# Front's input projection of a transformer-like block on one Trainium2 core: split fp32r operands in place of plain f32

## The reference, cut to what matters

```
h = x*(1 + scale) + shift ;  z = h @ w_in                      # [1024, P_IN], f32
mlstm:  q, k, v, o, gates   = z[:, 0:4*256], z[:, 1024:1040]
sgu:    u, v                = gelu(z[..., :256]), layer_norm(gelu(z[..., 256:]))
conv:   a = z[..., :256] * sigmoid(z[..., 256:]); 31-tap depthwise convolution in rows of 64 tokens,
        layer norm, silu
s5:     16 groups of a diagonal complex recurrence (64 states, two directions), driven by z[..., -256:]
```

## Time and profile before

| | |
|---|---|
| runs, us | 2306.5 (median), 2300.97, 2306.6 |
| profiled execution: span, us | 2301.7 (the page has no other time of it) |
| PE, DVE, ACT, POOL busy, us | 2196.2 (95%), 1350.5 (59%), 816.3 (35%), 333.9 (15%) |
| L1070, Front's tiles, PE busy us | 169.1, 384 records for 192 matmuls |
| DMA, mean | 94 GB/s |

### The profile page before, as it was taken

The page is one execution under the profiler, slowest core; times in us unless marked ns, Lnnn a source line. Parts: engine busy times, 40 slices in busy tenths (PEclk is TensorE's granted clock), DMA queues, the critical chain, the costliest instruction groups (busy, mean ns, idle before and its releaser), DMA issues. The chain is left out here.

```text
span 2301.7 us, 26756 instructions
## 1 busy us (share of the span) xinstructions
PE 2196.2 (95%) x10489; PEld 1634.2 (71%) x10489; DVE 1350.5 (59%) x2051; ACT 816.3 (35%) x1394; POOL 333.9 (15%) x257
## 2 busy tenths in 40 slices
PE   6999998878999999999999889999999999999999
PEld 3454764466778888888888668996768977444887
DVE  3829948576897655555455685317856387567210
ACT  3100113362562333333434352326544333446110
POOL 1000000031234322220000100004200000364000
PEclk9999999989999999999999999999999999999999
DMA  8531018304534322226534221100131210113331
GB/s 280 168 89 64 28 46 274 128 20 147 150 107 126 96 85 86 84 89 240 183 123 134 65 91 47 37 1 19 62 90 56 56 37 19 74 35 109 83 85 52
DMA packets 215428, 216.76 MB, mean 94 GB/s; under 512 B 18850, under 2 KB 171738, under 8 KB 214376
## 3 DMA queue, kind: packets, MB, share of 16 engines
q1 hardware_dynamic: 200076, 196.57, 27.3%
q0 software_dynamic: 3344, 12.58, 1.5%
q10 hardware_dynamic: 11884, 5.91, 0.9%
HBM read 172.12 MB, written 41.74 MB: 93 GB/s over the span
## 5 line engine op out<-in xcount | busy, mean ns | idle before, releaser
L2360 PE MATMUL bk_in<-t_part,a 128*128 128x512 f32 x1272 | 294.6, 390 | 1.3 <-DVE arena L2835 0.9
L2360 PEld LDWEIGHTS bk_in<-t_part,a 128*128 128x128 f32 x1272 | 238.4, 188 | 53.1 <-issue 3.0
L2379 PE MATMUL bk_in<-hid_part,b_part 128*128 128x512 f32 x1056 | 242.0, 391 | 3.1 <-DVE b_part L2710 3.1
L2379 PEld LDWEIGHTS bk_in<-hid_part,b_part 128*128 128x128 f32 x1056 | 198.1, 188 | 46.3 <-DVE b_part L2710 3.9
L1070 PE MATMUL fr_ps<-arena,work 128*128 128x512 f32 x384 | 169.1, 601 | 5.0 <-DMA work<-in_w_in 5.0
L3166 PE MATMUL bk_in<-h_part,sj_part 128*128 128x512 f32 x576 | 136.0, 396 | 6.7 <-DVE h_part L2870 5.2
L1070 PEld LDWEIGHTS fr_ps<-arena,work 128*128 128x128 f32 x384 | 73.5, 193 | 96.1 <-issue 91.0
L2360 PE MATMUL ml_o<-t_part,a 128*128 128x512 f32 x576 | 134.8, 389 | 0.0
L3166 PEld LDWEIGHTS bk_in<-h_part,sj_part 128*128 128x128 f32 x576 | 108.4, 190 | 33.8 <-issue 6.2
L2360 PEld LDWEIGHTS ml_o<-t_part,a 128*128 128x128 f32 x576 | 108.1, 188 | 22.4
L2443 ACT ACTIVATE a<-s_raw 128x512 fp32r<-128x512 f32 x88 | 55.6, 632 | 166.7 <-PE bk_in L2360 96.9
(11 more groups left out here) (703 smaller groups left out, 4042.4 us busy)
## 6 DMA issues: line engine op xcount, KB each, us to landing
work<-in_w_mod SPq DMA_DIRECT2D x24, 1024.0 KB, 8.1
w_raw<-in_w_ffn_out SPq DMA_DIRECT2D x43, 512.0 KB, 3.7
work<-in_w_in SPq DMA_DIRECT2D x25, 512.0 KB, 4.0
g_raw<-in_w_ffn_in SPq DMA_DIRECT2D x24, 512.0 KB, 3.9
hid_raw<-kept_hid SPq DMA_DIRECT2D x22, 512.0 KB, 4.9
w_raw<-in_w_in SPq DMA_DIRECT2D x20, 512.0 KB, 3.7
work<-in_w_out SPq DMA_DIRECT2D x8, 1024.0 KB, 7.2
kept_hid<-arena SPq DMA_DIRECT2D x26, 256.0 KB, 2.2
```

What stands on the lines that cost most here:

```text
L2360: mm = pe.matmul(bank, ring[n % 4][a][:, k, :], moving[:, b, k, :], start=(opens and k == 0 and j == 0), stop=(k == HK - 1 and j == 2), sk ...
L2379: mm = pe.matmul(pi[:, m, :], w_part[n % 2][:, a, at:at + P], hid_part[k][:, b, :], start=(k == 0 and j == 0), stop=(k == FT - 1 and j == 2))
```

## The change

Every tile becomes two (24 pieces: 12 for the first 512 tokens, then 12 for the others, each loading its 512 KB of weights anew, ring of 3). For each piece ScalarE rounds the weights to fp32r (`upper`) and GpSimd subtracts to get the rest (`lower`; half of piece 0 is VectorE's). h of one half of the tokens is held as its rounded part and its rest (`part`), made by ScalarE, and by VectorE and GpSimd. TensorE makes three fp32r products in place of each f32 one. The second half of x is modulated in place by ScalarE meanwhile, and `part` is filled again while tile 11 runs. As `part` lies where hT was, hT is made once more for the jobs after the tiles: its first half from x loaded back, its second from x loaded into its place, by ScalarE (even k) and GpSimd (odd k).

Moved with it: `turn_rates` runs ahead of tile 0; `impulses` is split in two (after tiles 8 and 9), and both directions of `V.T` share one place, so the second waits for the shifted copies of the first; `turn_inputs` after tiles 10 and 13; x is kept in DRAM by three DMAs; the loads of `wt` and `wd` come later; the convolution waits for `s.free` 16.

Left out of the diff: lines taken out (they are the kernel's above), semaphore names, `x_of(h, k)` in place of `xT` in the stage before, the assertion on sizes.

```diff
     z += 2 * DT * S5P
...
+    V.p = [A.view(z + i * DT, DT) for i in range(9)] + [A.view(M_SMALL + i * DT, DT) for i in range(13)] + \
+        [A.view(WR0 + 10368 + HALF, DT), A.view(M_SMALL + 13 * DT, DT)]
     assert z + 9 * DT <= SV0
...
+    V.wv = [A.view(WR0 + 4 * T + i * 2048, DT, S5L * S5P) for i in range(2)]
+    V.T = [A.view(SV0, S5G, P) for d in range(2)]
     V.Kb = A.view(U50, S5G, P)
...
+    slot_at = (WR0, WR0 + 2 * T, WR0 + 8 * T + 128)
+    piece = [rounded(nc, S, f"fw{i}", at, 2, KT, P) for i, at in enumerate(slot_at)]
+    piece_raw = [A.view(at + T, KT, P) for at in slot_at]
+    part = rounded(nc, S, "fr_h", H0, KT, 2, HALF)
+    part_raw = A.view(H0, KT, 2, HALF)
+    x0 = A.view(X0, KT, HALF)
+    N_PIECES = 2 * Z_TILES
+    BY_POOL = ((2, 5), (1, 3, 5, 7))
+    by_dve = [[k for k in range(KT) if k not in some] for some in BY_POOL]
+
+    first_done = 2 * len(by_dve[0]) + 1
 
     n_tok = W_MIX + 16 + W_MIX
...
+                sp.dma_start(kept_half[0], x0).then_inc(s.kept, 16)
+                sp.dma_start(kept_half[1][:, 0, :], S.x_of(1, 0)).then_inc(s.kept, 16)
+                sp.dma_start(kept_half[1][:, 1:, :], A.view(X0 + 4608, KT - 1, HALF)).then_inc(s.kept, 16)
 
                 for d in range(2):
                     sp.wait_ge(p.zeros, 2)
...
@@ -1028,10 +1045,18 @@
...
+                sp.wait_ge(p.spilled, 16)
+                sp.wait_ge(s.kept, 48)
+                sp.dma_start(x0, kept_half[0]).then_inc(s.kept, 16)
...
+                for a, b, off, n in ((0, 256, O_V, 256), (256, 272, O_G, 16), (272, 528, O_B + W_MIX, 256)):
+                    sp.dma_start(wt[:, :, a:b], w[:, :, off:off + n]).then_inc(s.wt, 16)
...
+                sp.wait_ge(s.kept, 64)
+                sp.dma_start(S.hT[:, :, cut[1]], kept_half[1]).then_inc(s.kept, 16)
+                sp.dma_start(wd, w[:, :, O_D:O_D + W_MIX]).then_inc(s.wd, 16)
...
+                    if n == 0:
+                        pe.wait_ge(s.h_d, first_done)
+                    pe.wait_ge(s.lo, n + 1)
+                    if n >= 4:
+                        pe.wait_ge(s.free, n - 3)
+                    half = n // Z_TILES
+                    for k in range(KT):
+                        if n % Z_TILES == 0:
+                            by_pool = BY_POOL[half]
+                            if k in by_pool:
+                                pe.wait_ge(s.h_p, (1 + half) * len(BY_POOL[0]) + by_pool.index(k) + 1)
+                            else:
+                                pe.wait_ge(s.h_d, (first_done if half else len(by_dve[0])) + by_dve[half].index(k) + 1)
+                        for j, (a, b) in enumerate(THREE):
+                            mm = pe.matmul(pm[:, n % 4, :], piece[n % 3][:, a, k, :], part[:, k, b, :],
+                                           start=(k == 0 and j == 0), stop=(k == KT - 1 and j == 2))
+                        if n % Z_TILES == Z_TILES - 1 and k < KT - 1:
+                            mm.then_inc(s.freed, 1)
+                    mm.then_inc(s.done, 1)
 
                 def job(n):
                     sta, mov, rows, cols, kind, _ = jobs[n]
...
+                        pe.wait_ge(s.hc, KT)
...
+                        if n == 0:
+                            pe.wait_ge((s.raw_a, s.raw_p)[k % 2], k // 2 + 1)
...
+                def impulses(d):
...
@@ -1202,7 +1238,8 @@
...
+                turn_rates()
+                tile(0)
...
@@ -1211,14 +1248,17 @@
...
+                for n in range(1, 9):
...
+                impulses(0)
+                tile(9)
+                impulses(1)
+                tile(10)
...
+                for n in range(11, 14):
+                    tile(n)
+                turn_inputs(1)
+                for n in range(14, N_PIECES):
...
@@ -1247,18 +1287,63 @@
 
             @block.gpsimd
             def _(pool):
...
+                def lower(n):
+                    pool.wait_ge(s.hi, n + 1)
+                    cols = slice(KT // 2, KT) if n == 0 else slice(0, KT)
+                    pool.tensor_tensor(piece[n % 3][:, 1, cols, :], piece_raw[n % 3][:, cols, :],
+                                       piece[n % 3][:, 0, cols, :].bitcast(F32), ALU.subtract).then_inc(s.lo, 1)
+
+                for k in BY_POOL[0]:
+                    pool.tensor_scalar(part_raw[:, k, 1, :], S.x_of(0, k), S.sc1[:, k, 0:1], S.mod[:, k, 0:1], ALU.mult,
+                                       ALU.add).then_inc(s.h_p, 1)
+                for i, k in enumerate(BY_POOL[0]):
+                    pool.wait_ge(s.h_p, i + 1)
+                    pool.wait_ge(s.h_a, k + 1)
+                    pool.tensor_tensor(part[:, k, 1, :], part_raw[:, k, 1, :], part[:, k, 0, :].bitcast(F32), ALU.subtract)\
+                        .then_inc(s.h_p, 1)
+                for n in range(2):
+                    lower(n)
                 pool.memset(V.K, 0.0).then_inc(p.zeros, 1)
+                lower(2)
                 pool.memset(V.Kb, 0.0).then_inc(p.zeros, 1)
+                for n in range(3, Z_TILES + 1):
+                    lower(n)
+                for k in BY_POOL[1]:
+                    pool.wait_ge(s.h_a, KT + k + 1)
+                    pool.tensor_tensor(part[:, k, 1, :], S.x_of(1, k), part[:, k, 0, :].bitcast(F32), ALU.subtract)\
+                        .then_inc(s.h_p, 1)
+                for n in range(Z_TILES + 1, N_PIECES):
+                    lower(n)
+                pool.wait_ge(s.kept, 64)
+                for k in range(1, KT, 2):
+                    if k < KT - 1:
+                        pool.wait_ge(s.freed, KT + k)
+                    else:
+                        pool.wait_ge(s.done, J0)
+                    pool.tensor_scalar(S.hT[:, k, cut[0]], x0[:, k, :], S.sc1[:, k, 0:1], S.mod[:, k, 0:1], ALU.mult,
+                                       ALU.add).then_inc(s.raw_p, 1)
+                pool.wait_ge(s.kept, 80)
+                for k in range(1, KT, 2):
+                    pool.tensor_scalar(S.hT[:, k, cut[1]], S.hT[:, k, cut[1]], S.sc1[:, k, 0:1], S.mod[:, k, 0:1],
+                                       ALU.mult, ALU.add).then_inc(s.raw_p, 1)
 
             @block.scalar
             def _(act):
...
+                def modulated(out, k, x):
+                    return nc.scalar.activation(out, x, ACT.Identity, bias=S.mod[:, k, 0:1], scale=S.sc1[:, k, 0:1])
+
+                def upper(n):
+                    act.wait_ge(loaded[n % 3], 16 * (n // 3) + 16)
+                    nc.scalar.activation(piece[n % 3][:, 0, :, :], piece_raw[n % 3], ACT.Copy).then_inc(s.hi, 1)
+
+                act.dma_start(piece_raw[0], columns_of(0)).then_inc(loaded[0], 16)
+                for k in range(6):
+                    modulated(part[:, k, 0, :], k, S.x_of(0, k)).then_inc(s.h_a, 1)
+                upper(0)
+                for k in range(6, KT):
+                    modulated(part[:, k, 0, :], k, S.x_of(0, k)).then_inc(s.h_a, 1)
+                act.dma_start(piece_raw[2], columns_of(2)).then_inc(loaded[2], 16)
+                upper(1)
                 act.wait_ge(p.in_dt, 16)
                 for e in range(2):
                     half = slice(64 * e, 64 * e + 64)
...
@@ -1268,13 +1353,37 @@
...
+                def take(n):
+                    m = tiles[n % Z_TILES]
+                    act.wait_ge(s.done, n + 1)
+                    nc.scalar.activation(S.z[:, m, cut[n // Z_TILES]], pm[:, n % 4, :], funcs[m]).then_inc(s.free, 1)
+
+                for n in range(N_PIECES):
+                    if n == Z_TILES - 1:
+                        for k in range(KT):
+                            if k < KT - 1:
+                                act.wait_ge(s.freed, k + 1)
+                            else:
+                                act.wait_ge(s.done, Z_TILES)
+                            act.wait_ge(s.x1, k + 1)
+                            nc.scalar.activation(part[:, k, 0, :], S.x_of(1, k), ACT.Copy).then_inc(s.h_a, 1)
+                    if n == N_PIECES - 1:
+                        act.wait_ge(s.kept, 64)
+                        for k in range(0, KT, 2):
+                            act.wait_ge(s.freed, KT + k)
+                            modulated(S.hT[:, k, cut[0]], k, x0[:, k, :]).then_inc(s.raw_a, 1)
+                    take(n)
+                    if n + 3 < N_PIECES:
+                        act.dma_start(piece_raw[n % 3], columns_of(n + 3)).then_inc(loaded[n % 3], 16)
+                    if n + 2 < N_PIECES:
+                        upper(n + 2)
+                    if 1 <= n <= KT:
+                        if n == 1:
+                            act.wait_ge(s.kept, 48)
+                        modulated(S.x_of(1, n - 1), n - 1, S.x_of(1, n - 1)).then_inc(s.x1, 1)
+                act.wait_ge(s.kept, 80)
+                for k in range(0, KT, 2):
+                    modulated(S.hT[:, k, cut[1]], k, S.hT[:, k, cut[1]]).then_inc(s.raw_a, 1)
...
@@ -1430,6 +1540,8 @@
...
+                            if d and b == 0:
```

(70 more changed lines are left out.)

50 lines of the change are left out of this document (13 added, 37 removed).

## The result

| | before | after |
|---|---|---|
| median, us | 2306.55 (2300.97 to 2309.81, 4 runs) | 2399.15 (2394.95 to 2405.5, 4 runs) |
| ratio | | 1.0402, 95% interval 1.0382 to 1.0422 |
| span of the profiled execution, us | 2301.7 | 2396.8 |

The change makes the kernel 4% slower: 92.6 us, where 30.5 were forecast. The direction was right, the size was not, and the time lies outside the range.

The account below looks back on a forecast made before the run. It took TensorE's and VectorE's chains in Front as level, with VectorE's deciding: 15.0 + 15.4 + 2 + 1 = +33 us, giving 2335 from the span or 2339 from the median; it said 2337, range 2309 to 2354.

Parts of the forecast that it names:

- The convolution: Front's taps on VectorE: seven lowers beside them add 15.4 us, GpSimd's scalings of plain h 2; end at 284.8.
- (b): Rival: GpSimd held up by taps, tiles with table loads late, TensorE idle before tile 15; +44, 2350; chance 0.17 including slower fp32r.
- at their 1.20 us pitch beside GpSimd's lowers: Sign against the forecast: convolution taps keep their pace while GpSimd subtracts, pointing to a level or faster kernel.
- c or d: Two rivals: level, little lost per lower, 2302 us, chance 0.10; faster, lowers fit VectorE's gaps, 2291 us, chance 0.07.
- twice the weight traffic is hidden: Front's tiles: 24 weight pieces of 512 KB, each needing about 2 of a tile's 5.46 us, delay nothing.
- The start: Before tile 0: scalings, subtractions and half pieces on VectorE and GpSimd move the first product from 48.91 to 56.
- TensorE's part: Front's projection: 576 fp32r products at 0.2273 us, 5.46 us a tile, 34 us less over 24 tiles.
- VectorE's first stretch and the wait in impulses(0): Nine lowers add 19.8 us to VectorE's work, ending at 128.6 instead of 112.0; TensorE idles about 17 us.
- From there to the convolution: From VectorE's copy through tile 15: waits and tiles sum to 63.3 us; convolution starts at 191.9, 15.0 later.
- A faster projection alone gives almost nothing: Front: TensorE's and VectorE's chains are level at 284, so shortening TensorE's products alone hardly moves the squares.
- The rest: After the convolution: rotations, centering, squares and later jobs follow as before, 32.4 us later, plus 1 for a colder clock.
- or the squares no longer right behind VectorE's centering: Sign against the forecast, at the end of Front's VectorE chain: TensorE's squares no longer directly follow the centering.

Follow-up runs that it names:

- the gaps: The changed kernel, but every fourth convolution tap waits for the tap right before it; measured 2355.94 us, ratio 1.0203 to the kernel before.

## Why the prediction was wrong

**The step that failed is "The convolution".** It put lowers 17 to 23 beside the taps at 7 x 2.2 us and the taps' busy time at 85 to 90 us. It carried the exchange of turns from the earlier trace rows over to the taps. The taps stayed at 71.83 us and the cost went to the other engine: one lower of 68.6 us, TensorE idle for 73.0. The four subtractions of the earlier trace rows leave no gap either; what was different is that GpSimd asked there during the first of four, and in the taps during the seventh overlapping instruction, with 55 more to come. The earlier trace rows had 60 taps in 71.83 us, so 1.197 apart; one of them lasts 1.27 in the trace of before, which the prediction did not look up. That they overlap could have been seen; what it does to GpSimd in a long run, no row of before showed. The rival (b) came nearest: it had the cost come by way of GpSimd and TensorE, but with GpSimd "held up by a tap (1.2 us) each time", where it was held for the rest of the run. Of the named signs, taps "at their 1.20 us pitch beside GpSimd's lowers" came true, and the prediction read it as a sign of c or d, that is of a level or faster kernel. That the direction came out right is no merit of this step.

A smaller part of the same wait fails with "twice the weight traffic is hidden": piece 17 landed about 7 us too late for TensorE.

With the gaps the step would have held: 90.99 us of taps, 19.2 more, against 15.4 + 2 (the gaps' own 2 us are in it).

The Trainium skill (SBUF — State Buffer, "SBUF: two separate sides") says that whoever starts first has the shared pair for the whole instruction, and its "Summary: rules for kernel authors" that the second one "fully blocks until the first finishes". The first stretch agrees: 2.19 us lost to a lower of 2.40 (L860). In the taps the second one was blocked for 55 further instructions after the first had finished; there the measurement decides. Also GpSimd's one-input scaling was blocked. The Trainium skill (same page, "Who interferes with whom") covers this: by it a VectorE instruction with two SBUF inputs contends with a GpSimd instruction that reads SBUF.

Point by point, the rest:

- *The start.* Forecast 56, measured 58.31: VectorE's six subtractions took 7.98 us, not 0.62 each; the collisions were heavier than the 3.5 us put in (52.5 to 56). In the run without subtractions tile 0 began at 54.91, so the lowers' share is 3.4.
- *TensorE's part.* 0.2273 us a product, measured 0.235 (33.86 for 144) and 0.245 (41.11 for 168, the clock cold at its start): a tile 5.6, not 5.46, 3 us in all.
- *VectorE's first stretch and the wait in impulses(0).* Forecast 128.6 and about 17 us idle; measured 130.7 and 16.05. Right, and shown to be the lowers: without them the wait is gone.
- *From there to the convolution.* Forecast 63.3 us, measured 73.8 (131.37 to 205.18). The granted clock is 0.70 and 0.68 in the two windows above, where the same windows of before have 1.00: between the levels of 1.2 and 2.4 GHz, TensorE having been idle for 16 us. Tile 9 took 7.01 and tile 10 7.70 against 5.6, and the second halves of both impulses 6.13 each against 3.24 for the first (the clock granted through both second halves was 0.50, the level of 1.2 GHz): about 9.3 us. The forecast had 3 for it, so this is about 6 of the 10.5. The waits for T and the shifts were 2.70 and 3.67 (forecast 1 to 2, and 5).
- *"A faster projection alone gives almost nothing."* It gives 13 us. The chains are level at the squares, but VectorE's chain itself hangs on TensorE's: turn_inputs(1) stands in TensorE's list, so a faster TensorE moves the convolution too (157 instead of 177).
- *The rest.* That the squares follow right behind VectorE's centering was not so in the changed kernel: VectorE was idle for 44.36 us, and TensorE ran from job 0 to the squares without a wait. The named sign "or the squares no longer right behind VectorE's centering" had come true: the centering began at 356.77 and the squares 17.4 us later.

## What to carry to other kernels

A price for two engines that share something holds only for the pattern in which it was read. Before work for GpSimd that reads SBUF is put beside VectorE instructions with two SBUF inputs, look at whether these begin before the last has ended, and for how many in a row. If GpSimd asks late in a long run of them, expect it to stand still to the run's end, and who waits for it to stand too. One wait for the preceding instruction at every fourth tap, about every 5 us, let GpSimd in each time, at about 0.1 us a gap. Here it was cheaper still to let VectorE do the work itself: 1.22 us for a lower, against 2.1 to 2.2 lost to one on GpSimd.

## What the runs showed of the hardware

- In the taps, a run of two-input VectorE instructions that overlap (1.197 us apart, 1.28 long; as tensor_tensor 1.14 and 1.22), GpSimd was shut out to the end of the run in five kernels (68.6, 65.0, 68.7, 65.0 and 36.3 us for one instruction), whatever VectorE's form (scalar_tensor_tensor or tensor_tensor, rows or flat) and GpSimd's (fp32r or f32 output, 128x1024 or 128x256).
- Overlap alone does not do it: in the kept traces GpSimd was let in when it asked during one of the first five overlapping instructions (2.39 us for the lower at 185.93), and held when it asked during the seventh or later. No run varied this by itself.
- It also happens to GpSimd's tensor_scalar with one input: four of 0.77 us took 39.26.
- VectorE loses nothing then: 71.83 us for 60 taps in the changed kernel, 71.84 in the kernel before with idle work beside them, and 71.83 without.
- A gap ended it within half a microsecond (the subtraction ended at 202.43, for a gap at about 202.0).
